# Two streams through a hybrid attention and S5 network on one core: early copies, tiles and splits written ahead of the table steps of a unit, sums' copies ahead of entering states, and the last group's outputs one in a unit

## The chip, the core and the metric

The kernel runs on one core of a Trainium2 chip. The metric is the device time of one execution in microseconds. Of the core's engines TensorE (PE, with its weight loads PEld), VectorE (DVE), ScalarE (ACT), GpSimd (POOL) and SyncE (SP, here only an issuer of DMAs) appear below.

## What is computed

One denoising step over two streams of 128 tokens, width 2048, through two layers. Layer 0 is attention, layer 1 a bidirectional diagonal state-space layer (S5). All weights are float32 and each is used once.

```python
def _pre(x, cond, g, w_ada, b_ada):
    shift, scale, gate = jnp.split(jax.nn.silu(cond) @ w_ada + b_ada, 3, axis=-1)
    h = _rmsnorm(x, g) * (1 + scale) + shift
    return h, gate
...
def _s5_layer(x, cond, p, init, return_state):
    h, gate = _pre(x, cond, g, w_ada, b_ada)
    u, z = jnp.split(h @ w_in, 2, axis=-1)
    ...
    hfr, hfi = _s5_scan(ug, a_re[0], a_im[0], log_dt[0], b_re[0], b_im[0], h0f)
    hbr, hbi = _s5_scan(ug[:, ::-1], a_re[1], a_im[1], log_dt[1], b_re[1], b_im[1], h0b)
    y = _s5_readout(hfr, hfi, c_re[0], c_im[0]) + _s5_readout(hbr, hbi, c_re[1], c_im[1])[:, ::-1]
    y = y.reshape(bsz, l, D_MODEL) + d_skip.astype(jnp.float32) * uf
    y = jax.nn.gelu(y).astype(x.dtype)
    y = y * jax.nn.sigmoid(y @ w_glu + b_glu)
    out = (y * jax.nn.silu(z)) @ w_out
    return x + gate * out
```

## The kernel before

**Units.** The large products (input and output projections of both layers, and the gated linear unit, GLU) are cut into 36 blocks of 512 output columns, and each block into 8 units of 256 input rows, 288 units in all, numbered k. Every engine's program is one Python loop over k, written out, and an engine executes its instructions in just that order. `place(k)` says which block and which of its units stands at k. A unit is 12 matmuls (`products`, lines 821 to 823): for two k tiles and two streams, the weight's high part with the activations' high part, the low part `wlo` with `xhi`, and `whi` with `xlo`.

**Splits.** ACT copies a unit's raw weights to their high part (`split`, line 1095) and DVE subtracts to get the low part (line 1495). From unit 12 on the split of unit k + 4 is written at unit k, and it waits until unit k has been multiplied. Raw weights are loaded by SP, one load for two units, into slots that free as units are multiplied.

**Early steps.** In the first 16 units the modulation of layer 0 is still being computed. TensorE multiplies the chunks of `w_ada` between units (`ada_early`, line 687); ACT copies a finished sum to `adasb` (`adasb_early`, line 1054); TensorE turns it to columns (line 693); DVE makes shift and scale of them and scales a transposed activation tile (`early_tiles`: lines 1481 to 1506), ACT takes its high part (line 1116) and DVE its low part `xlo` (line 1513). Tiles 2c and 2c + 1 are made at the end of unit 4c - 1.

**Table steps.** The tables of the S5 layer are made in 16 quarters n spread over the units by `table_units(n)`: five numbers, the units of `b_bar` (its two `b_table` halves, bt, follow one and two units later), of TensorE's transposes of bt (line 745, two units; ACT stages each half, bs, and stores it), of `c_table` (two units), of the band product (line 762) and of the diagonals.

**S5 steps.** Four groups w of 512 channels, in four quarters q each. `s5_sums` (TensorE line 939, then four ACT copies, lines 1188 and 1189, into sb) makes what a chunk of tokens adds to the state; DVE scans over the chunks; `s5_entering` (four ACT copies, lines 1204 to 1207, from sb into hy) lays out each chunk's entering state, `s5_outputs` (TensorE lines 958 and 962, then a GELU on ACT, line 1217, into ys) gives the outputs. Each sum uses the same two PSUM banks as the one before it, and each output the same one bank, so that TensorE waits for ACT's copies of the sum before (`s_Ssb`) and for ACT's GELU of the output before (`s_ysb`). S_AT, HY_AT and Y_AT are the first units of these steps for each group. A copy into sb of group w + 2 must follow the entering state of the same quarter of group w, which reads the same buffer. A group's outputs go to DRAM and come back transposed (Y, loaded by POOL); `transposed` (line 800) makes the activation tiles of the GLU of it, at the units of the fourth row of X_AT. Blocks 28 to 30 take turns from unit 224 to 247; tiles 6 and 7 are first used by units 242 and 243. After the last group's outputs POOL loads the GLU bias, the gates and the last norm's gains (lines 667, 562 and 670).

Of the kernel before, what the change touches and what calls it, by code (L numbers as in the profile page):

```python
# [57 lines left out]
def table_units(n):  # L58


    if n < 3:
        return ((3, 8, 6, 10, 10), (12, 15, 15, 19, 20), (17, 21, 20, 27, 28))[n]
    if n < 12:
        steps = ((1, 5, 4, 8, 9), (10, 14, 13, 17, 18), (17, 21, 20, 27, 28))[n % 3]
        return tuple(UB * 4 * (n // 3) + u for u in steps)
    steps = ((2, 6, 5, 9, 10), (8, 12, 11, 15, 16), (16, 20, 19, 22, 23), (22, 27, 25, 29, 30))[n - 12]
    return tuple(UB * B_OUT0 + u for u in steps)
# [23 lines left out]
def scan_plan():  # L91
# [4 lines left out]
    for k in range(sums[0], UB * B_END):  # L96
# [20 lines left out]
Y_AT = tuple(x + (4 if w < 2 else 3) for w, x in enumerate(HY_AT))  # L117
# [4 lines left out]
        tuple(UB * B_TURNS + u for u in (-5, -4, -2, 2, 7, 9, 14, 16)),  # L122
# [36 lines left out]
def quarters_at(starts, k):  # L159

    return [(w, q) for w, x in enumerate(starts) for q in range(4) if x + (q // 2 if w == NW - 1 else q) == k]

# [68 lines left out]
def build(nc, d):  # L231
    with ExitStack() as ctx:
# [447 lines left out]
        def _(pe):  # L680
# [286 lines left out]
            def s5_beside(k):  # L967
# [3 lines left out]
                for w, q in quarters_at(Y_AT, k):  # L971
# [35 lines left out]
        def _(act):  # L1007
# [218 lines left out]
            def s5_beside(k):  # L1226
# [6 lines left out]
                for w, q in quarters_at(Y_AT, k):  # L1233
                    s5_outputs(w, q)
                for w, q in quarters_at(HY_AT, k):
                    s5_entering(w, q)
                if s5_at(S_AT, 4, k):
                    s5_sums(*s5_at(S_AT, 4, k))
# [14 lines left out]
            for k in range(NU):  # L1253
# [7 lines left out]
                if u == 0 and ada_beside(b - 1) is not None:  # L1261
# [3 lines left out]
                    af(adasb[:, ada_slot(b)], ps[:, 4], ACT.Copy).then_inc(s_adasb, 1)  # L1265
                if b < B_OUT0:
# [3 lines left out]
                if k < 12 and k % 2 == 1:  # L1270
                    adasb_early(k // 4 + 1, k // 2 % 2)
                if k < 12 and k % 4 == 3:
                    split(k + 1)
                    split(k + 2)
                    early_tiles(k // 4 + 1)
                    split(k + 3)
                    split(k + 4)
# [56 lines left out]
        def _(dve):  # L1334
# [296 lines left out]
            def early_tiles(c):  # L1631
# [4 lines left out]
                modulated(0, 2 * c)  # L1636
                for g in (2 * c, 2 * c + 1):
                    low(0, g)

# [3 lines left out]
            for k in range(NU):  # L1643
# [13 lines left out]
                if k in YZ_AT:  # L1657
# [6 lines left out]
                    dve.wait_ge(s_yz, w + 1)  # L1664
                if b < B_OUT0:
                    attention(b // 4, b % 4, u)
                tables(k)
                if k < 12 and k % 4 == 3:
                    split(k + 1)
                    split(k + 2)  # L1670
                    early_tiles(k // 4 + 1)
                    split(k + 3)
                    split(k + 4)
# [144 lines left out]
```

## Time and profile before

| | |
|---|---|
| median of 3 runs | 1159.76 us (1158.07 to 1163.18) |
| the profiled execution | 1162.38 us |
| its span in the profile | 1160.4 us |
| TensorE busy | 1090.1 us, 94% of the span |
| DVE, ACT, POOL busy | 65%, 49%, 19% |
| mean granted TensorE clock | 0.974 of full speed |

The span runs from the first to the last recorded instruction; what lies around it is 2.0 us. TensorE's busy time is no measure of its speed, since its matmuls overlap. The profile also says for each instruction how long its engine stood idle ahead of it and which instruction of which engine ended that.

### The profile page before, as it was taken

Reading aid. Unit: us, or ns where it says so; the run is one execution under the profiler, and the core shown is the slowest. Engines: PE = TensorE matmul, PEld = TensorE weight load, DVE = VectorE, ACT = ScalarE, POOL = GpSimd, SP = SyncE. Lnnn points to the kernel's source line nnn. Section 1 sums busy time; section 2 is a strip of 40 time slices with the busy share of each in tenths; the row PEclk is TensorE's granted clock in tenths of the full one; section 3 lists DMA queues with packets and bytes.
Section 4 is the critical chain, followed back from the end, with each engine's and each line's share of the span. In section 5 each row is a group of like instructions: output and inputs, shape, how many; then the busy total and the mean of one; then the engine's idle time right before and its main releaser. Section 6 shows DMA issues by size and latency. Waiting matters only on the chain.

```text
span 1160.4 us, 17361 instructions
## 1 busy us (share of the span) xinstructions
PE 1090.1 (94%) x6786; PEld 825.6 (71%) x6786; DVE 757.7 (65%) x1209; ACT 568.8 (49%) x800; POOL 219.2 (19%) x378
## 2 busy tenths in 40 slices
PE   2998899999999999999999989999898998999997
PEld 0455677677777777778777657888686876888885
DVE  4353765766565765677687876369967796476665
ACT  4433434433433444435444346566668586355452
POOL 2010230343122511222134431100020202100000
PEclk9799899999999999999999989999898998999998
DMA  9999687889879997876598867877473767765552
GB/s 372 402 421 419 247 317 267 326 326 346 324 279 377 347 338 261 335 268 224 234 376 336 337 246 290 268 247 238 161 242 122 247 225 273 260 253 181 182 186 104
DMA packets 63457, 325.04 MB, mean 280 GB/s; under 512 B 9392, under 2 KB 16176, under 8 KB 31248
## 3 DMA queue, kind: packets, MB, share of 16 engines
q1 hardware_dynamic: 42800, 265.85, 61.5%
q0 software_dynamic: 12944, 46.94, 11.4%
q10 hardware_dynamic: 7632, 11.15, 2.7%
q8 instruction: 54, 0.88, 0.3%
q14 instruction: 27, 0.22, 0.1%
HBM read 295.55 MB, written 28.34 MB: 279 GB/s over the span
## 4 chain that ended last, share of the span: by engine, by line
PE 76%; DVE 9%; DMA 6%; ACT 6%; issue 3%; ACTq 0%; DVEq 0%
PE ps L821 20%; PE ps L823 18%; PE ps L822 18%; PE ps L687 7%; DMA raw<-in_w 3%; DVE wlo L1495 3%; PE ps L939 2%; ACT whi L1095 2%; PE ps L962 1%; PE ps L800 1%; PE ps L762 1%; DMA araw<-in_wada 1%; DMA gT<-in_gT 1%; PE ps L745 1%; ACT hy L1206 1%
## 5 line engine op out<-in xcount | busy, mean ns | idle before, releaser
L1495 DVE TENSOR_TENSOR wlo<-raw,whi 128x1024 fp32r<-128x1024 f32 x284 | 346.9, 1227 | 291.1 <-ACT whi L1095 286.9
L1095 ACT ACTIVATE whi<-raw 128x1024 fp32r<-128x1024 f32 x284 | 298.3, 1058 | 431.4 <-PE ps L823 403.9
L821 PE MATMUL ps<-whi,xhi 128*128 128x512 f32 x1136 | 465.6, 410 | 6.5 <-DVE xlo L1513 4.6
L822 PE MATMUL ps<-wlo,xhi 128*128 128x512 f32 x1152 | 455.0, 395 | 0.0
L823 PE MATMUL ps<-whi,xlo 128*128 128x512 f32 x1136 | 448.5, 395 | 0.0
L821 PEld LDWEIGHTS ps<-whi,xhi 128*128 128x128 f32 x1136 | 216.6, 191 | 92.7 <-issue 27.9
L823 PEld LDWEIGHTS ps<-whi,xlo 128*128 128x128 f32 x1136 | 216.4, 190 | 48.1
L822 PEld LDWEIGHTS ps<-wlo,xhi 128*128 128x128 f32 x1152 | 220.0, 191 | 41.4
L687 PE MATMUL ps<-araw,cT 128*32 128x512 f32 x640 | 78.6, 606 | 1.9 <-DMA araw<-in_wada 1.9
L687 PE MATMUL ps<-raw,cT 128*32 128x512 f32 x128 | 20.2, 734 | 28.3 <-DMA gT<-in_gT 16.1
L687 PEld LDWEIGHTS ps<-araw,cT 128*32 128x32 f32 x640 | 16.9, 110 | 39.6 <-issue 30.8
L629 POOL DMA_DIRECT2D ctab<-ctab_scratch x16 | 8.6, 541 | 190.8 <-PE ps L962 190.8
L1607 DVE TENSOR_TENSOR t<-coef,sb 128x256 f32<-128x256 f32 x66 | 27.9, 422 | 23.8 <-ACT sb L1189 22.6
L1612 DVE TENSOR_TENSOR sb<-sb,t 128x128 f32<-128x128 f32 x140 | 40.4, 292 | 4.6
L939 PE MATMUL ps<-utf,btab 64*128 64x64 f32 x512 | 35.1, 291 | 8.0 <-ACT sb L1189 8.0
L939 PEld LDWEIGHTS ps<-utf,btab 64*128 64x128 f32 x512 | 32.9, 204 | 13.1 <-issue 12.9
L1513 DVE TENSOR_TENSOR xlo<-ps,xhi 128x512 fp32r<-128x512 f32 x40 | 27.4, 688 | 19.7 <-ACT xhi L1116 19.5
L1116 ACT ACTIVATE xhi<-ps 128x512 fp32r<-128x512 f32 x40 | 23.7, 593 | 29.6 <-DVE ps L1506 19.4
L523 POOL COPY bbf<-bb 64x256 f32<-64x256 f32 x16 | 12.2, 762 | 121.5 <-DVE bb L1410 108.3
L687 PEld LDWEIGHTS ps<-raw,cT 128*32 128x32 f32 x128 | 3.2, 119 | 38.5 <-DMA gT<-in_gT 16.1
L499 POOL DMA_DIRECT2D par<-in_par x16 | 8.7, 547 | 114.3 <-DVE bt L1422 114.0
L531 POOL TENSOR_SCALAR ce<-par 128x128 f32<-128x128 f32 x32 | 28.8, 902 | 2.9
(227 smaller groups left out, 1100.3 us busy)
## 6 DMA issues: line engine op xcount, KB each, us to landing
raw<-in_w SPq DMA_DIRECT2D x144, 1024.0 KB, 5.7
araw<-in_wada SPq DMA_DIRECT2D x80, 1024.0 KB, 8.8
raw<-in_wada SPq DMA_DIRECT2D x16, 1024.0 KB, 9.8
ctab_scratch<-ce POOLq DMA_DIRECT2D x16, 512.0 KB, 8.4
btab_scratch<-bs ACTq DMA_DIRECT2D x32, 256.0 KB, 5.8
btab<-btab_scratch SPq DMA_DIRECT2D x16, 512.0 KB, 3.9
ctab<-ctab_scratch POOLq DMA_DIRECT2D x16, 512.0 KB, 4.8
par<-in_par POOLq DMA_DIRECT2D x32, 128.0 KB, 6.6
```

What stands on the lines that cost most here:

```text
L531: last = nc.gpsimd.tensor_scalar(ce[:, 1, j], par[:, 3], -1.0, None, ALU.mult)
L687: last = mm(ps[32 * j:32 * j + 32, bank], cT32[:, c * CK + j], rhs[:, j * BN:(j + 1) * BN], start=c == 0, stop=c == NCK - 1)
L821: mm(acc, xhi[:, kt, st], hi[:, k], start=kt == 0, stop=False)
L822: mm(acc, xhi[:, kt, st], wlo[:, slot, k0 % 2, k], start=False, stop=False)
L823: last = mm(acc, xlo[:, kt, st], hi[:, k], start=False, stop=kt == KT - 1)
L939: last = mm(ps[:, (4, 7)[e], c0:c0 + M2], btab[h, q, k, ri], utf[h, w, 4 * q + k], start=True, stop=True)
L1095: af(whi_at(k).rearrange("p k c -> p (k c)"), src, ACT.Copy).then_inc(s_hi, 1)
L1116: af(xhi[:, 2 * g:2 * g + 2].rearrange("p k s c -> p (k s c)"), ps[:, x_bank(n)], ACT.Copy).then_inc(s_xhi, 1)
L1495: tt(wlo[:, slot, k % 2].rearrange("p k c -> p (k c)"), src, whi_at(k).rearrange("p k c -> p (k c)").bitcast(F32), ALU.subtract).then_inc( ...
L1513: tt(xlo[:, 2 * g:2 * g + 2].rearrange("p k s c -> p (k s c)"), ps[:, x_bank(n)], xhi[:, 2 * g:2 * g + 2].rearrange("p k s c -> p (k s c)" ...
L1607: last = tt(t, coef[:, w], now.unsqueeze(1).to_broadcast([P, 2, 2, 2 * GW]), ALU.mult)
L1612: last = tt(nxt, nxt, t[:, :, half], ALU.add)
```

## The change

It changes the order in which instructions are written, and no instruction's work:

- In units 1 to 11, the copy of the early sums, the early tiles and the splits are written ahead of the table steps of their unit. On DVE one split now lies between the scaling of the tiles and their low parts; on ACT one split is written ahead of the tiles and three behind them, where there were two and two.
- The table of units for quarter 1 has its first number at 11 where it was 12.
- On ACT, `s5_sums`' copies are written ahead of `s5_entering` of the same unit.
- The last group's outputs start at unit 231, one in a unit up to 234 (they were two at unit 230 and two at 231), and tiles 6 and 7 of the GLU are transposed at units 241 and 242 (they were at 238 and 240).

```diff
--- before.py
+++ after.py
@@ -59,7 +59,7 @@
 
 
     if n < 3:
-        return ((3, 8, 6, 10, 10), (12, 15, 15, 19, 20), (17, 21, 20, 27, 28))[n]
+        return ((3, 8, 6, 10, 10), (11, 15, 15, 19, 20), (17, 21, 20, 27, 28))[n]
     if n < 12:
         steps = ((1, 5, 4, 8, 9), (10, 14, 13, 17, 18), (17, 21, 20, 27, 28))[n % 3]
         return tuple(UB * 4 * (n // 3) + u for u in steps)
@@ -114,12 +114,12 @@
 
 
 S_AT, HY_AT, SCAN = scan_plan()
-Y_AT = tuple(x + (4 if w < 2 else 3) for w, x in enumerate(HY_AT))
+Y_AT = tuple(x + (4, 4, 3, 4)[w] for w, x in enumerate(HY_AT))
 
 
 X_AT = ((), tuple(UB * B_OUT0 + u for u in (-4, -2, -1, 1, 1, 2, 3, 4)),
         tuple(UB * B_IN1 + u for u in (0, 0, 0, 1, 2, 3, 4, 5)),
-        tuple(UB * B_TURNS + u for u in (-5, -4, -2, 2, 7, 9, 14, 16)),
+        tuple(UB * B_TURNS + u for u in (-5, -4, -2, 2, 7, 9, 17, 18)),
         tuple(UB * B_OUT1 + u for u in (-6, -5, -4, -3, -2, -1, 3, 4)))
 X_BANK = ((5, 6, 5, 6, 5, 6, 5, 6), (4, 4, 7, 7, 5, 6, 7, 5), (6, 7, 5, 6, 7, 5, 6, 7), (5, 7, 4, 7, 7, 7, 7, 7),
           (7, 5, 6, 7, 5, 6, 7, 5))
@@ -159,6 +159,11 @@
 def quarters_at(starts, k):
 
     return [(w, q) for w, x in enumerate(starts) for q in range(4) if x + (q // 2 if w == NW - 1 else q) == k]
+
+
+def outputs_at(k):
+
+    return [(w, k - x) for w, x in enumerate(Y_AT) if 0 <= k - x < 4]
 
 
 def ahead(k):
@@ -968,7 +973,7 @@
 
                 if k in U_AT:
                     s5_transposed(U_AT.index(k))
-                for w, q in quarters_at(Y_AT, k):
+                for w, q in outputs_at(k):
                     s5_outputs(w, q)
                 if s5_at(S_AT, 4, k):
                     s5_sums(*s5_at(S_AT, 4, k))
@@ -1230,12 +1235,12 @@
                 if k in U_AT:
                     for i in range(2):
                         s5_transposed(U_AT.index(k), i)
-                for w, q in quarters_at(Y_AT, k):
+                for w, q in outputs_at(k):
                     s5_outputs(w, q)
+                if s5_at(S_AT, 4, k):
+                    s5_sums(*s5_at(S_AT, 4, k))
                 for w, q in quarters_at(HY_AT, k):
                     s5_entering(w, q)
-                if s5_at(S_AT, 4, k):
-                    s5_sums(*s5_at(S_AT, 4, k))
                 if k == Y_AT[NW - 1] + 4:
                     act.wait_ge(s_fsT, 1)
                     act.wait_ge(s_y, 4 * NW)
@@ -1263,18 +1268,17 @@
                     if ada_order(b) > 2:
                         act.wait_ge(s_adafin, fins(b - 1))
                     af(adasb[:, ada_slot(b)], ps[:, 4], ACT.Copy).then_inc(s_adasb, 1)
+                if k < 12 and k % 2 == 1:
+                    adasb_early(k // 4 + 1, k // 2 % 2)
+                if k < 12 and k % 4 == 3:
+                    split(k + 1)
+                    early_tiles(k // 4 + 1)
+                    for x in range(k + 2, k + 5):
+                        split(x)
                 if b < B_OUT0:
                     attention(b // 4, b % 4, u)
                 tables(k)
                 s5_beside(k)
-                if k < 12 and k % 2 == 1:
-                    adasb_early(k // 4 + 1, k // 2 % 2)
-                if k < 12 and k % 4 == 3:
-                    split(k + 1)
-                    split(k + 2)
-                    early_tiles(k // 4 + 1)
-                    split(k + 3)
-                    split(k + 4)
                 if u == UB - 1:
                     if b < B_GLU and not B_OUT0 <= b < B_IN1:
                         act.wait_ge(s_wused, k + 1)
@@ -1628,15 +1632,17 @@
                         if step == NCH - 1:
                             scanned(w)
 
-            def early_tiles(c):
+            def early_tiles(c, unit=None):
+
                 dve.wait_ge(s_adaE, c + 1)
                 cols = [ps[:, 7, 16 * c + 8 * i:16 * c + 8 * i + 8].rearrange("p (k s) -> p k s", s=NS) for i in range(2)]
                 shift_or_scale(cols, 0, c, 4 * c, 4, s_adaEout)
                 dve.wait_ge(s_adaEout, c + 1)
                 modulated(0, 2 * c)
+                if unit is not None:
+                    split(unit)
                 for g in (2 * c, 2 * c + 1):
                     low(0, g)
-
             for k in range(4):
                 split(k)
             early_tiles(0)
@@ -1662,15 +1668,13 @@
                     cols = slice(w * BN, (w + 1) * BN)
                     tt(WA[:, :, cols], WA[:, :, cols], Y[:, :, cols], ALU.mult).then_inc(s_yz, 1)
                     dve.wait_ge(s_yz, w + 1)
+                if k < 12 and k % 4 == 3:
+                    early_tiles(k // 4 + 1, k + 1)
+                    for x in range(k + 2, k + 5):
+                        split(x)
                 if b < B_OUT0:
                     attention(b // 4, b % 4, u)
                 tables(k)
-                if k < 12 and k % 4 == 3:
-                    split(k + 1)
-                    split(k + 2)
-                    early_tiles(k // 4 + 1)
-                    split(k + 3)
-                    split(k + 4)
                 if u == UB - 1:
                     if B_OUT0 <= b < B_IN1:
                         if b == B_OUT0:
```

On DVE, the piece around the end of unit 11 (in the changed kernel line numbers are 4 or 5 higher). Names are tiles: wlo is the low part of a split, shT, modt and gsT the shift and scale, xlo a tile's low part, bands the diagonals of unit 10, bb the first table step of quarter 1. Before:

```order
L1495 TENSOR_TENSOR wlo<-raw,whi 128x1024 x2
L1481 TENSOR_TENSOR shT<-ps,bT 128x8
L1484 TENSOR_TENSOR modt<-ps,bT 128x8
L1486 SCALAR_TENSOR_TENSOR gsT<-modt,gT 128x8
L1506 TENSOR_SCALAR ps<-ps,gsT,shT 128x128 x4
L1513 TENSOR_TENSOR xlo<-ps,xhi 128x512 x2
L1495 TENSOR_TENSOR wlo<-raw,whi 128x1024 x3
L1405 TENSOR_TENSOR bb<-ff,par 128x128
```

and now:

```order
L1458 TENSOR_TENSOR bands<-bands,ps 128x2x16
L1459 TENSOR_TENSOR bands<-bands,dm 128x2x16
L1485 TENSOR_TENSOR shT<-ps,bT 128x8
L1488 TENSOR_TENSOR modt<-ps,bT 128x8
L1490 SCALAR_TENSOR_TENSOR gsT<-modt,gT 128x8
L1510 TENSOR_SCALAR ps<-ps,gsT,shT 128x128 x4
L1499 TENSOR_TENSOR wlo<-raw,whi 128x1024
L1517 TENSOR_TENSOR xlo<-ps,xhi 128x512 x2
L1499 TENSOR_TENSOR wlo<-raw,whi 128x1024 x3
L1409 TENSOR_TENSOR bb<-ff,par 128x128
```

The two splits that stood ahead of the shift and scale are behind them, one of them between the scaling and the low parts.

On ACT, at units 207 and 208 (S5 groups 1 and 3). hy is an entering state, sb what the sums' copies write, WA the SiLU of the evacuated block. Before:

```order
L1095 ACTIVATE whi<-raw 128x1024
L1204 ACTIVATE hy_109<-h_113 64x16x2
L1205 ACTIVATE hy_109<-h_113 64x16x2
L1206 COPY hy_109<-sb 64x16x62
L1207 COPY hy_109<-sb 64x16x62
L1188 COPY sb<-ps 64x2x4x32x2
L1189 COPY sb<-ps 64x2x4x32x2
L1188 COPY sb<-ps 64x2x4x32x2
L1189 COPY sb<-ps 64x2x4x32x2
```

and now:

```order
L1100 ACTIVATE whi<-raw 128x1024
L1193 COPY sb<-ps 64x2x4x32x2
L1194 COPY sb<-ps 64x2x4x32x2
L1193 COPY sb<-ps 64x2x4x32x2
L1194 COPY sb<-ps 64x2x4x32x2
L1209 ACTIVATE hy_109<-h_113 64x16x2
L1210 ACTIVATE hy_109<-h_113 64x16x2
L1211 COPY hy_109<-sb 64x16x62
L1212 COPY hy_109<-sb 64x16x62
```

The four copies into sb have changed places with the four copies into hy.

On ACT, units 229 to 233: ys is the GELU of one quarter's outputs, xhi a tile's high part. Before:

```order
L1095 ACTIVATE whi<-raw 128x1024 x2
L1217 ACTIVATE ys<-ps 128x4x64 x2
L1116 ACTIVATE xhi<-ps 128x512
L1095 ACTIVATE whi<-raw 128x1024
L1217 ACTIVATE ys<-ps 128x4x64 x2
L1223 DMA y_scratch<-ys 128x1x256 x4
L1095 ACTIVATE whi<-raw 128x1024
L1116 ACTIVATE xhi<-ps 128x512
```

and now:

```order
L1100 ACTIVATE whi<-raw 128x1024 x2
L1121 ACTIVATE xhi<-ps 128x512
L1100 ACTIVATE whi<-raw 128x1024
L1222 ACTIVATE ys<-ps 128x4x64
L1100 ACTIVATE whi<-raw 128x1024
L1222 ACTIVATE ys<-ps 128x4x64
L1121 ACTIVATE xhi<-ps 128x512
L1100 ACTIVATE whi<-raw 128x1024
L1222 ACTIVATE ys<-ps 128x4x64
L1100 ACTIVATE whi<-raw 128x1024
L1222 ACTIVATE ys<-ps 128x4x64
L1228 DMA y_scratch<-ys 128x1x256 x4
```

Between two GELUs there is now a split in every case, and the tile of unit 231 and three splits stand ahead of the first.

## Rows read from the trace of the kernel before

**Rows 1.** The page: the span, and three groups of instructions.

```profile
span 1160.4 us, 17361 instructions
L1495 DVE TENSOR_TENSOR wlo<-raw,whi 128x1024 fp32r<-128x1024 f32 x284 | 346.9, 1227 | 291.1 <-ACT whi L1095 286.9
L1095 ACT ACTIVATE whi<-raw 128x1024 fp32r<-128x1024 f32 x284 | 298.3, 1058 | 431.4 <-PE ps L823 403.9
L1513 DVE TENSOR_TENSOR xlo<-ps,xhi 128x512 fp32r<-128x512 f32 x40 | 27.4, 688 | 19.7 <-ACT xhi L1116 19.5
```

**Rows 2.** Timeline of the early stage: start, length in us, engine, line, operation, idle before.

```profile
103.94 0.60 ACT L1054 ACTIVATE adasb<-ps 128x512 f32<-128x512 f32 x1 [0.46 <-ACT bs L1065]
...
104.59 1.92 PE L687 MATMUL ps<-raw,cT 128*32 128x512 f32 x16 [2.63 <-ACT adasb L1054]
...
113.05 1.87 PE L693 MATMUL ps<-sel,adasb 128*128 128x2 f32 x16
...
117.51 1.37 DVE L1506 TENSOR_SCALAR ps<-ps,gsT,shT 128x128 f32<-128x128 f32 x4
...
120.35 0.79 PE L821 MATMUL ps<-whi,xhi 128*128 128x512 f32 x1 [2.56 <-DVE xlo L1513]
...
127.09 0.28 DVE L1405 TENSOR_TENSOR bb<-ff,par 128x128 f32<-128x128 f32 x1
...
135.59 0.66 PE L745 MATMUL ps<-ident,bt 128*128 128x128 f32 x4 [2.66 <-DVE bt L1422]
```

**Rows 3.** Engines by stretch: busy us (count), then TensorE's granted clock, DMA share, GB/s.

```profile
110.00:115.00 5.00, 5.00 (x61) 3.56 (x50) 0.62 (x3) 2.35 (x5) 0.00 (x0) 1.00 1.02 425
833.50:840.30 6.80, 6.80 (x41) 5.97 (x41) 6.29 (x17) 6.64 (x11) 0.00 (x0) 0.51 0.23 78
980.20:987.00 6.80, 5.12 (x56) 4.66 (x57) 3.81 (x4) 2.52 (x5) 0.00 (x0) 0.50 0.12 51
```

**Rows 4.** Groups of instructions of the stretch from 820 to 1000 us.

```profile
L1206 ACT COPY hy<-sb 64x992 f32<-64x992 f32 x16 | 17.4, 1089 | 0.2
L1205 ACT ACTIVATE hy<-h 64x32 f32<-64x32 f32 x16 | 3.7, 229 | 0.2
```

**Rows 5.** Timeline of the sums and entering states.

```profile
833.25 1.08 PE L939 MATMUL ps<-utf,btab 64*128 64x64 f32 x8 [3.58 <-ACT sb L1189]
...
841.48 1.06 ACT L1095 ACTIVATE whi<-raw 128x1024 fp32r<-128x1024 f32 x1 [1.10 <-PE ps L823]
...
852.43 0.38 ACT L1217 ACTIVATE ys<-ps 128x256 f32<-128x256 f32 x1
...
891.04 3.42 PE L939 MATMUL ps<-utf,btab 64*128 64x64 f32 x32 [2.00 <-ACT sb L1189]
...
899.25 1.06 ACT L1095 ACTIVATE whi<-raw 128x1024 fp32r<-128x1024 f32 x1 [2.29 <-PE ps L823]
```

**Rows 6.** Timeline: starts of units 212, 213, 229 and 230, then the last outputs.

```profile
907.39 0.50 PE L821 MATMUL ps<-whi,xhi 128*128 128x512 f32 x1
...
912.05 0.50 PE L821 MATMUL ps<-whi,xhi 128*128 128x512 f32 x1
...
969.31 0.39 PE L821 MATMUL ps<-whi,xhi 128*128 128x512 f32 x1
...
972.03 0.39 PE L821 MATMUL ps<-whi,xhi 128*128 128x512 f32 x1
...
979.47 1.06 ACT L1095 ACTIVATE whi<-raw 128x1024 fp32r<-128x1024 f32 x1
...
981.88 1.12 PE L958 MATMUL ps<-kd,utf 64*64 64x64 f32 x16 [5.28 <-ACT ys L1217]
...
1002.10 0.47 PE L821 MATMUL ps<-whi,xhi 128*128 128x512 f32 x1
```

**Rows 7.** DMAs issued from 999 to 1007 us: count, KB, us from issue to landing.

```profile
gfin<-in_g_fin POOLq DMA_DIRECT2D x1, 1024.0 KB, 21.5
raw<-in_w SPq DMA_DIRECT2D x1, 1024.0 KB, 12.0
```

## The prediction

> **What bounds the kernel now.** The page's engine table shows TensorE busy almost throughout, but its matmuls overlap, so the first view that says something is the timeline of TensorE with the idle time ahead of each instruction. One unit of 12 matmuls takes 969.31 to 972.03 = 2.72 us when nothing waits, and a unit with an S5 output behind it 907.39 to 912.05 = 4.66, so an output costs 1.94 [rows 6]. The 288 units alone are 288 x 2.72 = 783 us of the span of 1160.4 [rows 1]. What a new order can win is the time in which TensorE waits, and it does so in three places that this change touches:
>
> A, the early stage: 2.63 us for the copy adasb, 2.56 for the low part of tile 6, 2.66 for the bt table [rows 2].
> B, the sums: 3.58 at 833.25 and 2.00 at 891.04, both for ACT's copies sb [rows 5].
> C, the last outputs: 5.28 at 981.88 for the GELU ys [rows 6].
>
> The second view is the table by stretches, for the clock. TensorE was granted 0.51 of full speed, 1.2 instead of 2.4 GHz, from 833.5 to 840.3, right after the 3.58 us wait, and 0.50 from 980.2 to 987.0, around the 5.28 us wait [rows 3]. So a long wait is paid twice: 6.8 us at half speed, all of it worked through, is 3.4 us lost. The wait of 2.63 us at 104.59 [rows 2] was not followed by it: 110 to 115 shows 1.00 [rows 3].
>
> **The change part by part.** No instruction is added or removed; every term is a wait that gets shorter or longer.
>
> *A.* On ACT the copy adasb at 103.94 goes ahead of one staged copy and the wait on it, 0.60 + 0.46 = 1.1 us [rows 2], so TensorE's wait of 2.63 becomes 1.5 and the columns (113.05, 1.87 long) end at 113.8 instead of 114.9. DVE scaled the tile at 117.51 only because two splits of 1.23 each [rows 1] stood ahead of it; now it starts on the columns, and with half a microsecond for the three small operations the scaling runs from 114.4 to 115.8. Then one split (1.23) while ACT takes the high part, and the low part (0.69, rows 1 again): 117.7, where TensorE started unit 12 at 120.35. That is 2.6 us. DVE then owes, up to the end of the second bt half: a low part 0.69, three splits 3.7, the six small operations that begin at 127.09 (0.28 each, 1.7), and two splits and two halves of three 0.69 operations, 2.5 + 4.1; with about 1.1 of waits on ACT's parts, 13.8 us: 131.5, against 135.59 [rows 1, 2]. TensorE waits there still, about 2.5 us, but 4.0 earlier. Term A is **4.0**. It rests on DVE, which has nothing idle in that stretch; were the copy's 1.1 lost, it is 3.0; if the half-speed stretch after the wait disappears as well (a bt wait of 2.5 is near the 2.63 that did without), up to 5.4. The lower bound is 0: from 110 to 115 the DMA engines are full (share 1.02, 425 GB/s) [rows 3], and if the weights of units 12 to 15 land no earlier than they are used now, nothing moves. I keep 4.0, because DVE made the splits of 12 and 13 before 117.51, so that those weights were there; what moves is work done after they land.
>
> What pays for A: the second half of `c_table` for quarter 0 goes behind the splits of units 10 and 11 on DVE, to about 105.5 (these splits end near 103.4, and it is three operations of 0.69). TensorE's band product needs it at the end of unit 10, about 108: a cover of 2 to 3 us, and one for one beyond it. The first `b_bar` moves behind splits too, and POOL, which fills ce and issues loads, is later by up to 20 us; it is next needed at unit 15, near 131.
>
> *B, groups 0 and 2 (units 197 to 201).* An entering state is two copies of 1.09 and two of 0.23 [rows 4], 2.7 us with the gaps. With the sums' copies ahead of it, the sum that TensorE began at 833.25 can begin at 830.6. But ACT is the bound here: it is busy 98% of the stretch at 833.5 [rows 3], and up to the GELU that ends at 852.43 + 0.38 = 852.81 its one pause is the 1.10 us at 841.48 in which it waited for TensorE [rows 5]. TensorE's second output needs that GELU. All work is the same in a new order, so only the 1.1 us go: TensorE gains 2.7 at first and gives back all but **1.1** at unit 201. Without the half speed TensorE is at that output some 4 us earlier and released 1.1 earlier, so a wait of about 2.9 arises there. Bounds: +1.2, and 3.4 less, -2.2, if half speed follows it.
>
> *B, groups 1 and 3 (units 207 to 211).* The copies that released TensorE at 891.04 end 2.7 us earlier. Here ACT has room: its split at 899.25 waited 2.29 us for TensorE [rows 5], and more behind it, so the gain stays. The half-speed time I leave as it is: the first wait of this stretch goes, but the other grows to about 3.6 us. Term **2.7**, bounds 2.3 (ACT's room) and 6.0 (one stretch at half speed, 3.4, less).
>
> Behind the copies of sums stand the entering states, 2.5 us later; outputs read them four units later, more than 10 us, which covers it.
>
> *C.* From the start of unit 230 (972.03) to that of unit 235 (1002.10) it is 30.1 us [rows 6]. Without waits: five units 13.6, four outputs 7.8, two tiles' transposes of at most the 0.66 of the four at 135.59 [rows 2], say 0.8 for both: 22.2. The new order asks the first GELU of ACT later: after 979.47 two splits (2.1), the tile's high part 0.6, a split 1.06, the GELU 0.38, 983.5. TensorE reaches the second output at 972.03 + 3 x 2.72 + 1.94 + 0.4 = 982.5, and waits 1.0. The next two outputs have a full unit ahead of them, 2.7 us, where a split and a GELU take 1.5. So 23.2 instead of 30.1: 6.9 gained. Against it, tiles 6 and 7 are now transposed right ahead of the last unit before the ones that use them. For tile 7, DVE has behind unit 241: a high part 1.06 (ACT), a split 1.23, the product of WA and Y over 1024 columns 1.2, its low part 0.69, together 4.2; unit 242 with its transposes is 3.1. TensorE waits 1.1 at unit 243. Term C is **5.8**. Bounds: 6.9 if that wait is covered; 3.7 if the weights of unit 244, whose split stands ahead of tile 6 on ACT, take the 12.0 us of a load issued under the POOL loads [rows 7] instead of about 10: then tile 6 is late too.
>
> Sum: 4.0 + 1.1 + 2.7 + 5.8 = 13.6 us, against the profiled execution's own 1162.38 (span 1160.4, 2.0 around it): 1148.8. That execution lies 2.6 above the median of the runs, 1159.76, so the median should be **1146.2**.
>
> **A rule weighed.** The rows say that after 3.58 us of waiting the clock was 0.51, and after 2.63 us still 1.00. The Trainium skill, "TensorE: Matmul & The Clock Gate", part 1 on the clock gate, has it that the throttled state is the default and that only activity releases it, on a grid of time that does not start with the kernel. By that, which of two similar waits is punished is chance. By the rows, the sum keeps as much half-speed time in A and B as now; by the rule, the waits left in B (2.4, 2.9 and 3.6 us) could each bring one. That is the second rival.
>
> **The rivals.**
> 1. *ACT and DVE are the bound and only hand the wait on.* In B and A no work is taken from them. For it: ACT's one pause of 1.1 us ahead of 852.81. Against it: 2.29 us of pause at 899.25 [rows 5]. If B gives nothing, 1162.4 - 9.8 = 1152.6, median 1150.0; if A gives nothing instead (loads late, share 1.02), 1149.9 to 1150.2. Chance 0.22 for either.
> 2. *The waits stay long enough to halve the clock each time.* In B two more stretches of 6.8 us, 3.4 us each less the waits that they shorten, take back term B's 3.8 and up to 2 more: median 1150 to 1152. Chance 0.10. The skill's clock page, same part, is behind this one.
> 3. *A table step or tile becomes the wait.* c_table behind the splits in A, or tiles 6 and 7 in C, late by 8 us together: median within 0.5% of now, 1154 to 1158. Chance 0.10.
> 4. *Slower.* POOL's loads (Y, bias, gates, gains: 4.5 MB) are issued as now when the last outputs are stored, which is two to three units later in the order of units. gfin took 21.5 us to land among them [rows 7]. If the weights of unit 244 landed like that and not like the 12.0 us, tile 6 would wait behind the split on ACT for 9 us more. Against the 10 us assumed, each us to landing costs one: from 24 us on the 13.6 are gone, and at 32 us the median is 1168. Against it: weights come on another queue and took 12.0 at the height of that traffic. Chance 0.03. The Trainium skill, "DMA: Bandwidth & Descriptors", on queues, rings and completion order, says that a DMA engine takes turns between the queues that have work; the two rows of group 7 agree.
>
> **How the numbers follow.** The forecast has 0.55, its own range 1142 to 1149. Rivals 1 and 2 reach to 1153, and its upper ends (A 5.4, B 1.2 + 6.0, C 6.9, 19.5 in all) to 1140: the range is 1140 to 1153, and leaves out rivals 3 and 4 and some of the tail. A change of 0.5%, 5.8 us, is about what a measurement of this kernel tells from none. Faster by more: 0.55 + 0.22 + 0.10 = 0.87; within it: rival 3, 0.10; slower by more: 0.03.
>
> **What would show it.** A: unit 12 starts near 117.8, the bt wait ends near 131.5. B: the sum after unit 198 starts 2.7 earlier relative to its unit, then TensorE waits nearly 3 us for the GELU at the output of unit 201; ACT shows no pause between. At unit 210 ACT's wait for TensorE is gone or short. C: outputs one a unit, a wait of about 1 us at the second, clock 1.00 around it, and a wait of about 1 us at unit 243. The prediction is wrong if half-speed stretches move to 848 to 855, if the wait for xlo at 242 or 243 is over 3 us with a weight load ahead of it, or if the band product at unit 10 waits for ce.

## The result, and the profile after

The kernel after takes 1156.08 us (median of 20 runs, 1149.81 to 1161.92), the kernel before, run beside it, 1160.63 (20 runs, 1158.07 to 1164.45). The ratio is 0.9948, interval 0.9936 to 0.9960: 6.0 us less, not 13.6. It is outside the range, and it lies where rival 3 was put (1154 to 1158). The runs after spread over 12 us, those before over 6. That made me look for two cases among the executions, but by itself it proves nothing: 29 runs of the kernel before in the first set of experiments spread over 11.7 us (1156.10 to 1167.76).

The profiled execution took 1160.52 us, 4.4 above the median, so it is one of the slower executions. Its page begins so:

```profile
span 1158.7 us, 17360 instructions
PE 1087.1 (94%) x6786; PEld 822.4 (71%) x6786; DVE 757.3 (65%) x1209; ACT 568.3 (49%) x800; POOL 216.5 (19%) x378
```

**Place A.** The timeline of TensorE (start, length, line, and in brackets the idle time ahead and what ended it): unit 12, and the transposes of bt ahead of unit 16.

```profile
116.45 0.50 PE L826 MATMUL ps<-whi,xhi 128*128 128x512 f32 x1 [0.99 <-DVE xlo L1517]
...
133.20 1.11 PE L750 MATMUL ps<-ident,bt 128*128 128x128 f32 x4 [5.22 <-DVE bt L1426]
```

Unit 12 starts at 116.45 where it started at 120.35 [rows 2]: 3.9 us, even more than forecast. But the wait for bt ends at 133.20 instead of 135.59: 2.4 us of it are kept, and the wait has grown from 2.66 to 5.22. ACT and DVE in the same stretch show why:

```profile
125.64 2.01 ACT L1100 ACTIVATE whi<-raw 128x1024 fp32r<-128x1024 f32 x2 [5.61 <-DMA raw<-in_w]
```

```profile
122.95 0.29 DVE L1414 TENSOR_TENSOR bb<-bb,m 128x128 f32<-128x128 f32 x1
126.80 1.23 DVE L1499 TENSOR_TENSOR wlo<-raw,whi 128x1024 fp32r<-128x1024 f32 x1 [3.56 <-ACT whi L1100]
127.94 0.69 DVE L1419 TENSOR_TENSOR bt<-pw,bb 128x512 f32<-128x512 f32 x1
...
132.46 0.69 DVE L1426 TENSOR_TENSOR bt<-bt,m 128x512 f32<-128x512 f32 x1
```

ACT's split of unit 16 waited 5.61 us for its weights, DVE's half of that split waited for ACT, and the first half of `b_table`, which needs neither, stands behind it. DVE is idle 3.56 us between `b_bar` and the split: the pause that the prediction said was not there. The load of these weights, in the stretch from 110 to 113.2 of before and of after (KB, us to landing):

```profile
raw<-in_w SPq DMA_DIRECT2D x1, 1024.0 KB, 11.6
...
raw<-in_w SPq DMA_DIRECT2D x1, 1024.0 KB, 15.3
```

It was asked for at 110.31 where it was asked for at 112.62, and yet it landed later, at 125.62 instead of 124.27: in this stretch, where the DMA engines are full [rows 3], asking sooner did not bring it sooner.

**Place B.** Two rows of TensorE, an output behind unit 201 and a sum behind unit 209:

```profile
850.47 0.68 PE L963 MATMUL ps<-kd,utf 64*64 64x64 f32 x16 [2.58 <-ACT ys L1222]
...
887.41 0.91 PE L944 MATMUL ps<-utf,btab 64*128 64x64 f32 x6 [3.44 <-ACT sb L1194]
```

The waits are those forecast, 2.9 and 3.6.

**Place C.** TensorE's outputs of the last group, tile 7's transposes and unit 242, then ACT and DVE just ahead of them:

```profile
976.56 0.68 PE L963 MATMUL ps<-kd,utf 64*64 64x64 f32 x16
...
981.22 0.68 PE L963 MATMUL ps<-kd,utf 64*64 64x64 f32 x16
...
986.25 0.68 PE L963 MATMUL ps<-kd,utf 64*64 64x64 f32 x16
...
1017.90 1.09 PE L805 MATMUL ps<-ident,Y 128*128 128x128 f32 x4 [5.20 <-DVE xlo L1517]
1018.64 0.78 PE L826 MATMUL ps<-whi,xhi 128*128 128x512 f32 x1
```

```profile
1014.84 1.06 ACT L1100 ACTIVATE whi<-raw 128x1024 fp32r<-128x1024 f32 x1 [6.91 <-DMA raw<-in_w]
1015.80 0.58 ACT L1121 ACTIVATE xhi<-ps 128x512 fp32r<-128x512 f32 x1
```

```profile
1015.93 1.23 DVE L1499 TENSOR_TENSOR wlo<-raw,whi 128x1024 fp32r<-128x1024 f32 x1 [6.74 <-ACT whi L1100]
1017.07 0.68 DVE L1517 TENSOR_TENSOR xlo<-ps,xhi 128x512 fp32r<-128x512 f32 x1
```

The outputs wait for nothing any more, where the kernel before waited 5.28 us [rows 6]. Then the split of unit 244 waits for its weights, the high and low part of tile 6 stand behind it on both engines, tile 7 needs tile 6's bank, and TensorE waits 5.20 us. POOL's issues and the issues by line of two short stretches (KB, us to landing) tell what was ahead of those weights:

```profile
999.08 0.71 POOL L650 DMA_DIRECT2D Y<-y_scratch  x1 [29.46 <-DMA y_scratch<-ys]
999.84 0.56 POOL L672 DMA_DIRECT2D bglu<-in_b_glu  x1
```

```profile
bglu<-in_b_glu POOLq DMA_DIRECT2D x1, 1024.0 KB, 8.6
...
raw<-in_w SPq DMA_DIRECT2D x1, 1024.0 KB, 13.5
```

The weights were asked for at 1001.36, 1.5 us behind POOL's load of bglu, and landed 13.5 us later. Last the windows (length, busy time and count of each engine, granted clock, DMA share, GB/s) behind the three waits and around the outputs:

```profile
131.90:138.70 6.80, 5.50 (x16) 4.48 (x17) 5.66 (x7) 1.68 (x3) 4.30 (x7) 0.52 0.22 77
...
852.10:855.50 3.40, 3.40 (x16) 2.66 (x13) 2.66 (x8) 2.01 (x3) 0.53 (x1) 0.54 0.46 142
...
977.00:990.00 13.00, 13.00 (x174) 10.69 (x170) 9.51 (x9) 6.68 (x10) 0.00 (x0) 1.00 0.60 234
1015.90:1022.70 6.80, 4.80 (x14) 4.02 (x15) 4.78 (x5) 2.02 (x3) 0.00 (x0) 0.52 0.70 292
```

The half speed of before at the outputs [rows 3] is gone, and stands behind the three new waits shown here instead.

### The profile page after: what moved, and what is told of

It reads as the page before. It is cut to its first block, busy times and chain, and to the rows that moved or that the text cites. A ratio compares the mean times of both kernels' runs of the same rounds, so it can differ in the third digit from the quotient of the medians.

```text
span 1158.7 us, 17360 instructions
## 1 busy us (share of the span) xinstructions
PE 1087.1 (94%) x6786; PEld 822.4 (71%) x6786; DVE 757.3 (65%) x1209; ACT 568.3 (49%) x800; POOL 216.5 (19%) x378
## 3 DMA queue, kind: packets, MB, share of 16 engines
q0 software_dynamic: 12944, 46.94, 11.5%
## 4 chain that ended last, share of the span: by engine, by line
PE 72%; DMA 10%; DVE 8%; ACT 6%; issue 3%; ACTq 0%; DVEq 0%; SPq 0%
PE ps L826 19%; PE ps L828 18%; PE ps L827 18%; PE ps L692 7%; DMA raw<-in_w 4%; DVE wlo L1499 3%; DMA araw<-in_wada 2%; DMA raw<-in_wada 2%; ACT whi L1100 2%; PE ps L967 1%; PE ps L805 1%; PE ps L750 1%; PE ps L767 1%; DMA gT<-in_gT 1%; PE ps L944 1%
## 5 line engine op out<-in xcount | busy, mean ns | idle before, releaser
L805 PEld LDWEIGHTS ps<-ident,WA 128*128 128x128 f32 x128 | 16.4, 152 | 14.3 <-issue 10.8
```

Source lines behind the costliest of these rows:

```text
L805: last = tr(ps[:, x_bank(n), (2 * k + st) * P:(2 * k + st + 1) * P], src[:, st, (2 * g + k) * P:(2 * g + k + 1) * P], ident[:])
```

## The experiments

### The three parts, each alone

Each kernel is the one before with one part of the diff of the change: A (the order in the ACT and DVE loops, `b_bar` at 11), B (`s5_sums` ahead of `s5_entering` on ACT), C (`Y_AT`, `outputs_at`, and the last two entries of the tiles' row).

```diff
A -    return ((3, 8, 6, 10, 10), (12, 15, 15, 19, 20), ...
A +    return ((3, 8, 6, 10, 10), (11, 15, 15, 19, 20), ...   and early copies, tiles, splits ahead of tables(k)
B +                if s5_at(S_AT, 4, k): s5_sums(...)           ahead of the loop over s5_entering
C -        tuple(UB * B_TURNS + u for u in (-5, -4, -2, 2, 7, 9, 14, 16)),
C +        tuple(UB * B_TURNS + u for u in (-5, -4, -2, 2, 7, 9, 17, 18)),   and outputs_at(k)
```

> The kernel before with part A alone (early copies, tiles and splits ahead of the table steps, first b_bar at unit 11 instead of 12). The prediction's term says 4.0 us less than before (ratio 0.9966). Theory 1, that the gain of units 12 to 15 (3.9 to 5.0 us in the trace of after) is handed to a wait for the second bt half, which stands on DVE behind the split of unit 16 whose weights land at 125.6: 1.0 to 2.0 us (0.9983 to 0.9991), with a wait of over 4 us at the transposes of bt behind unit 15 and unit 17 some 1.5 us earlier. Theory 2, that what is lost there is one unlucky half-speed stretch: 4 to 5 us in the median of the runs, and in a profile without half speed after that wait.

> The kernel before with part B alone (copies of the sums ahead of the entering states on ACT). The prediction's term says 3.8 us less (0.9967). Theory 1, from the trace of after, where units 199 to 203 gave back all but -0.4 us of the 2.7 and units 207 to 211 kept 1.8: 1 to 2 us (0.998 to 0.999). Theory 2, half speed by chance: the two places differ between executions, and the median comes near 3.8.

> The kernel before with part C alone (last group's outputs one in a unit, tiles 6 and 7 ahead of units 241 and 242). The prediction's term says 5.8 us less (0.9950). Theory 1: the outputs give 6.7 us as forecast, and the transposes of tile 7 ahead of unit 242 then wait over 4 us for the low part of tile 6, which stands on ACT and DVE behind the split of unit 244, whose weights land late; with the half speed behind that wait, all of it is given back: -1.5 to +1.5 us (0.9987 to 1.0013). Theory 2, that the weights' landing varies with what the POOL queue does and this part on its own leaves the units later against the loads: 3 to 6 us less.

| part | ratio to before, interval | us, from the ratio | forecast |
|---|---|---|---|
| A | 0.9985, 0.9974 to 0.9997 | 1.7 (0.3 to 3.0) | 4.0 |
| B | 0.9977, 0.9963 to 0.9990 | 2.7 (1.2 to 4.3) | 3.8 |
| C | 0.9998, 0.9981 to 1.0015 | 0.2 (-1.7 to 2.2) | 5.8 |

Together 4.6 of the 6.0. A keeps its wait for bt, 4.08 us long:

```profile
132.64 0.69 PE L745 MATMUL ps<-ident,bt 128*128 128x128 f32 x2 [4.08 <-DVE bt L1421]
```

B fits its forecast within its interval, but 2.7 lies between the two theories named ahead of it (1 to 2, and near 3.8) and doesn't choose. C alone gives nothing in the ratio, but its 12 runs go from 1156.40 to 1164.72, and the profiled one is the quickest of them: there no wait stands ahead of unit 242, and the issue of the weights of unit 244, in a stretch at 1002.5, reads

```profile
raw<-in_w SPq DMA_DIRECT2D x1, 1024.0 KB, 4.8
```

POOL's bias load was issued at 1004.17 there, behind the weights. So the second theory, which expected the landing to vary, had a point, but not in the median, where the first has its number. From here on the question was that order.

### Tile 6 ahead of the split of unit 244

```diff
     last = UB * (B_END - 1)
+    if k in (240, 241):
+        return () if k == 240 else (244, 245)
     if k < last - 2:
```

> The kernel after with one exchange on ACT and DVE: the split of unit 244 stands behind the parts of tile 6 instead of ahead of them. The loads are not touched. Theory 1 (tile 6 was late only because it stood behind a split that waited 6.9 us for its weights): the wait of 5.2 us ahead of unit 242 goes or is under 1 us, unit 244 waits little, and the time is 5 to 8.5 us below that of after (0.993 to 0.9955 of it; 0.988 to 0.990 of before). The rival, that the weights are late for the units themselves: the wait moves to unit 244 or 245 and under 2 us are gained.

1154.79 us (6 runs, 1150.45 to 1157.73), ratio 0.9942, interval 0.9923 to 0.9962: 0.7 us below after, within the noise. The first theory asked for 5 to 8.5. Its profile (1150.93) happened to have the weights issued just ahead of POOL's loads too, so it could not tell; the forced pair below could.

### The same kernel, two more profiled executions

> The kernel after unchanged, one more profiled execution. If the order of the loads is what differs between executions of it: either POOL's loads are issued ahead of the weights of unit 244, these take over 11 us and unit 242 waits over 4 us, or behind them, these take about 5 us and no wait stands at unit 242, and the time is then 5 us or more below 1160.5. If the order is the same in every execution, the wait of 5.2 us is there again.

> The same as the look before, a third profiled execution of the kernel after.

1149.24 and 1150.75 us, with the kernel after unchanged. Of the first of these two (the second execution in the table below), TensorE ahead of unit 242 and what preceded it on ACT, and the issues of a stretch at 996.2:

```profile
1007.53 0.63 PE L805 MATMUL ps<-ident,Y 128*128 128x128 f32 x4
1007.91 0.47 PE L826 MATMUL ps<-whi,xhi 128*128 128x512 f32 x1
```

```profile
1004.47 1.06 ACT L1100 ACTIVATE whi<-raw 128x1024 fp32r<-128x1024 f32 x1 [1.66 <-PE ps L828]
1005.43 0.58 ACT L1121 ACTIVATE xhi<-ps 128x512 fp32r<-128x512 f32 x1
```

```profile
raw<-in_w SPq DMA_DIRECT2D x1, 1024.0 KB, 4.8
```

These weights were issued at 996.24, POOL's bglu at 997.37. No wait for tile 6, no half speed from 1003 to 1012. From the start of unit 241 to that of unit 243 it is 13.57 us in the first profile (1009.69 to 1023.26) and 7.35 in this one (1004.56 to 1011.91): 6.2 us, wait and half speed together, between the two orders of the loads within one kernel. The third execution has the same order, the good one with the weights ahead (weights at 997.17, bglu at 998.49). Part by part, by how much earlier than in the profile of before the units start (at unit 17; from there to 230; from 230 to 243):

| execution of after | A | to unit 230 (B) | C | sum |
|---|---|---|---|---|
| first, 1160.52 us | 1.6 | 1.4 | -1.2 | 1.7 |
| second, 1149.24 us | 3.2 | 4.1 | 5.7 | 13.1 |
| third, 1150.75 us | 4.2 | 3.1 | 4.8 | 12.1 |
| forecast | 4.0 | 3.8 | 5.8 | 13.6 |

So sums near the forecast's do occur in the quick executions; 5 of the 20 runs behind the median are below 1153 us. But each row is a difference of two single executions, and that of before was a slow one (1162.38). The profiles of B alone and C alone, which lack part A, start unit 17 also 1.6 and 2.0 us ahead of it. So this table does not show that A gives 3.2 or 4.2 us; only the terms of B and C come near their size by it.

The order of the two loads seems to hang on the last store of ys, for whose landing POOL's first load waits. In the first execution that store was issued at 995.24, ahead of the load of the weights of unit 242 (995.67), and landed 3.4 us later. In the second and third it was issued at 990.78 and 991.75, behind that load (990.55 and 991.48), and landed after 5.4 and 5.5 us, and POOL's loads with it came later. Of the other seven profiles with part C six fit this; in C alone the store was 0.2 us ahead of the load and took 6.3. No run forces this pair, so it is not shown to be the cause.

### The order of the loads, forced both ways

The first edit, on POOL, puts its loads of bias, gates and gains behind the weights of unit 244 (the load of Y stays ahead of them); the second, on SP, makes the weights wait until the last quarter of Y has landed, which puts them behind the issue of all of POOL's loads; the third is the second with the exchange of tile 6 and the split as above.

```diff
(later)   pool.wait_ge(s_y, 4 * NW)
(later)  +pool.wait_ge(s_wused, 239)
(later)   pool.dma_start(bglu[:], ...
(behind) +if g == 122:
(behind) +    sp.wait_ge(s_yin[3], 16)
(behind)  slot = w_slot(g)[0]
```

> The kernel after with one wait more on POOL: its loads of the bias, the gates, the gains and the store of the state wait until unit 238 is done, so that they are issued behind the load of the weights of units 244 and 245 and not just ahead of it. Theory (the traces of after, of C alone and of the run with tile 6 first differ in this order, by chance of when the store of the last output lands: with POOL's loads ahead the weights took 13.5 us, with them behind 4.7 and 4.8): the load takes about 5 us in every run, the wait ahead of unit 242 is gone, the runs lose their upper part, and the median is 3 to 5 us below that of after (ratio to before 0.990 to 0.992). The rival, that the spread comes from half-speed stretches elsewhere: the median stays within 1.5 us of after's.

> The kernel after with the load of the weights of units 244 and 245 forced behind POOL's loads (SP waits until the last quarter of Y has landed). If the order of these loads decides, this is the bad case in every run: the weights take 10 to 14 us, unit 242 waits 6 to 9 us for the low part of tile 6, part of it is followed by half speed, and the median is 3 to 6 us above after's (ratio to before 0.998 to 1.000). The rival, that it does not matter: within 1.5 us of after.

> The same forced order of loads, and the parts of tile 6 ahead of the split of unit 244 on ACT and DVE. If tile 6 was late only by its place behind the split, the wait ahead of unit 242 goes although the weights are as late; what is left is a wait of unit 244 itself, which starts about 5 us later: under 4 us, and the median is 3 to 6 us below that of the forced order alone. The rival, that the load is late for the units themselves whatever the order on ACT: under 2 us between the two.

| kernel | median us | ratio to before, interval | us less than before |
|---|---|---|---|
| after | 1156.08 | 0.9948, 0.9936 to 0.9960 | 6.0 |
| POOL's loads later | 1151.14 | 0.9920, 0.9905 to 0.9936 | 9.3 |
| weights behind | 1157.63 | 0.9968, 0.9955 to 0.9980 | 3.7 |
| weights behind, tile 6 first | 1158.32 | 0.9978, 0.9963 to 0.9993 | 2.6 |

The two kernels that differ from after by one wait each, on POOL or on SP, lie 5.6 us apart, and the kernel after lies between, as a mixture of the two orders should. The first is within what was expected; the second is 2.3 us above after where 3 to 6 were expected. The second edit also delays the weights themselves: they were asked for at 1006.22, 6 us behind the start of unit 238, and not at once as in after, so its wait is a longer one than the plain order makes. With POOL's loads later, the weights landed in 5.3 us and no wait stands ahead of unit 242. With the weights behind, TensorE waited 7.88 us; that row, and the row of the fourth kernel that takes its place:

```profile
1019.67 0.66 PE L807 MATMUL ps<-ident,Y 128*128 128x128 f32 x2 [7.88 <-DVE xlo L1519]
```

```profile
1026.26 0.79 PE L830 MATMUL ps<-whi,xhi 128*128 128x512 f32 x1 [4.52 <-DVE xlo L1521]
```

With tile 6 first, unit 242 starts without a wait and unit 243 waits 4.52 us for tile 7, which stands behind the splits of units 244 and 245 and is followed by half speed (0.67 from 1026 to 1031). In the median nothing is gained, where 3 to 6 us were expected. So by the medians the late landing costs as much with tile 6 ahead of the split as behind it. The profiles don't agree with that in full: from the start of unit 241 to that of unit 245 it is 21.67 us with the weights behind and 17.72 with tile 6 first, against 12.93 with POOL's loads later. The profile with tile 6 first is the slowest of its 12 runs (1165.04) and also has a wait of 5.38 us for Y ahead of unit 231, which is not part of the edit. Whether the exchange is worth something when the weights are late stays open; that their landing is what costs is shown by the first two edits.

### Both halves of b_table at once, ahead of the split of unit 16

```diff
-                        if k == units[0] + 1 + ri:
+                        if k == units[0] + (0 if n == 1 else 1 + ri):
                             b_table(n, ri)
```

> The kernel after with both halves of b_table of the second quarter right behind its b_bar on DVE at unit 11, ahead of the split of unit 16. Theory: the wait of 4 to 5 us at the transposes of bt behind unit 15 is not work of DVE but bt standing behind a split whose weights land at 125.6: it goes to under 1 us, unit 17 starts 3 to 4 us earlier than in after, and with a stretch at half speed less up to 3 us more; the time is 2 to 5 us below after (0.990 to 0.993 of before). The rival, that the early stage is bound by the DMA engines (share 1.0): the wait moves to the units 16 to 20 for their weights and under 1 us is gained.

> The kernel before with part A, and the two halves of b_table at unit 11, right behind the b_bar. Part A alone gave a ratio of 0.9985. If the place of bt behind the split of unit 16 took part A's gain, this one gives 5.3 us more, 7.0 us or 0.9940, and the trace shows no wait at the transposes of bt and full speed from 125 to 145. If the early stage hands the wait on to later weights: 0.997 to 0.9985.

On the kernel after: 1149.61 us, ratio 0.9902, interval 0.9886 to 0.9918, 5.3 us below after. On part A alone: 1153.84 us, ratio 0.9941, interval 0.9923 to 0.9959, the 0.9940 expected: 6.9 us from part A where it gave 1.7. The rival, a stretch bound by the DMA engines, falls: ACT still waited 5.93 us for the weights of unit 16, but no wait of TensorE followed from it. DVE's rows of the first kernel, TensorE's and two windows:

```profile
124.21 0.29 DVE L1414 TENSOR_TENSOR bb<-bb,m 128x128 f32<-128x128 f32 x1
124.54 0.69 DVE L1419 TENSOR_TENSOR bt<-pw,bb 128x512 f32<-128x512 f32 x1
...
128.20 0.69 DVE L1426 TENSOR_TENSOR bt<-bt,m 128x512 f32<-128x512 f32 x1
128.93 1.22 DVE L1499 TENSOR_TENSOR wlo<-raw,whi 128x1024 fp32r<-128x1024 f32 x1
```

```profile
129.06 0.60 PE L750 MATMUL ps<-ident,bt 128*128 128x128 f32 x4
130.29 0.47 PE L826 MATMUL ps<-whi,xhi 128*128 128x512 f32 x1 [0.64 <-ACT qkvz L1137]
```

```profile
120.00:130.00 10.00, 9.66 (x44) 7.54 (x43) 9.72 (x16) 4.07 (x6) 2.20 (x3) 1.00 0.89 361
130.00:140.00 10.00, 9.71 (x49) 8.06 (x50) 9.86 (x12) 7.13 (x11) 5.50 (x7) 1.00 0.72 248
```

The six operations of bt fill the time in which DVE waited, the transposes start at 129.06 without a wait (133.20 in after), and the clock stays at 1.00. So the gain is the wait and the half speed behind it; the runs don't part the two.

### Both edits together

> The kernel after with both edits that helped: the two halves of b_table right behind the b_bar at unit 11, and POOL's loads behind the load of the weights of unit 244. If the two losses are apart, their gains over after (5.3 and 3.3 us by the ratios) add: 8.6 us below after, ratio to before 0.9872, and a median near 1147. If the gain of the first came only because units then met POOL's loads at another moment, they don't add: 0.989 to 0.991.

1146.87 us (6 runs, 1144.03 to 1152.36), ratio 0.9889, interval 0.9864 to 0.9913: 12.9 us below before and 6.8 below after. The sum of the two, 8.6, is within the interval, and so is a loss of 2 us in the combination; these runs don't decide between them. The ratio expected if they add was 0.9872. It has the lowest median of the study and is clear of after, but not of the kernel with bt at once alone (ratio 0.9902), whose interval overlaps. That its median is about the predicted one is chance: it is another kernel.

## Why the prediction was wrong

**C, the step that failed most.** "3.7 if the weights of unit 244, whose split stands ahead of tile 6 on ACT, take the 12.0 us of a load issued under the POOL loads [rows 7] instead of about 10". The mechanism was named and its row read; its size was wrong twice. The weights took 13.5 us, so that TensorE waited 5.2 us for tile 6 where that sentence has about 2; and I gave that wait no half speed, though from 1015.9 to 1022.7 the clock was 0.52 with TensorE busy 4.80 us of it, so about 2.4 us more (half speed costs half of the busy time only). The term that the sum used, a landing of about 10 us, stands in no row: in the profile of before the load asked for at the start of unit 238 took 11.5 us. One figure for the landing was also the wrong idea: issued ahead of POOL's load of bglu the weights took 4.7 to 6.4 us in the profiles, behind it 10.4 to 13.5. The outputs themselves gave what was forecast: from unit 230 to unit 235 the profiles differ by 6.6 us (2.9 earlier at 230, 9.5 at 235), forecast 6.9. In the executions with the weights ahead, the only wait behind them is the 1.0 us at unit 243, as forecast (1.1). What decides is something that I had written under rival 4 as fixed, "issued as now when the last outputs are stored": in the profile of before POOL's loads were issued from 999 on and unit 238, at whose start the weights of unit 244 are asked for, began at 1010.75; in after unit 238 begins at 1001.17 and POOL's loads are still issued at 999 to 1001. The 9.5 us gained by the units brought the two together. With the good order forced, 9.3 us are gained; less A's 1.7 and B's 2.7, measured alone, that leaves 4.9 for C, of 5.8.

**A.** "It rests on DVE, which has nothing idle in that stretch" was wrong. The forecast let DVE work through its 13.8 us; after 122.95 it had work, but the next instruction in its order was a split whose weights had not landed. I had looked at the landing of the weights of units 12 to 15 (correctly: unit 12 gained 3.9 us) and not of unit 16, which landed no sooner (125.62, before 124.27) though all else had moved ahead. The first profile kept 2.4 us of 4.0, the wait grew to 5.22, and half speed (131.9 to 138.7) followed it; alone, the part gave 1.7. In the other two executions the wait for bt is 4.2 us as well and A's gain at unit 17 is 3.2 and 4.2, with as much half speed or half of it, so part of A's spread is the clock's. The edit with bt at once takes both away.

**B.** Right within what can be told: 2.7 (1.2 to 4.3) for 3.8. The waits were 2.58 and 3.44 for 2.9 and 3.6. Whether group 0 and 2 give 1.1 or lose hung on the clock: in the first profile half speed followed the wait of 2.58, and unit 203 starts 0.9 us earlier than before, where unit 198 started 1.6 earlier: a loss of 0.7. In the third execution of the same kernel the wait was 2.63 and 848 to 856 ran at 1.00.

**The rule weighed.** The forecast rested on one wait that was not punished, 2.63 us and then 1.00 [rows 3]. The profile of before has two more of that length in the same stage, 2.56 us at 120.35 and 2.66 at 135.59 [rows 2], and both went the other way:

```profile
120.00:123.30 3.30, 2.95 (x7) 2.38 (x8) 1.74 (x3) 3.27 (x6) 0.00 (x0) 0.50 1.01 416
137.00:140.40 3.40, 3.40 (x9) 2.52 (x8) 1.79 (x3) 1.08 (x2) 2.86 (x5) 0.50 0.36 121
```

So "a bt wait of 2.5 is near the 2.63 that did without" was no ground for a bound. Of the kernel after the rows say: 2.58 us of wait, then clock 0.54; 2.63 us at the same place in another execution, then 1.00. The Trainium skill, "TensorE: Matmul & The Clock Gate", part 1, has it that the grid is not tied to the kernel's start, so that the same wait may or may not be punished; the traces agree. I gave that rival 0.10 and left the forecast's half-speed time as it was, which was too kind for a change that leaves waits of 2.5, 2.9 and 3.6 us.

**The rivals.** Rival 3 came true in its time and in one of its two places, tiles 6 and 7; the other, `c_table`, didn't show: no wait for ce or at the band product. That its time was hit is in part luck: of the 7.6 us missing, 2.3 are A's and 1.1 B's, by the parts measured alone, and neither is a tile or `c_table` that came late. It should have had more than 0.10, since two steps of the sum named the same suspect. Rival 1's "loads late" is half of A. Rival 4 had the right transfer and overrated it.

## What to carry to other kernels

- When work is moved ahead, look past the wait that it removes for the next load that the sooner consumers ask for, and for everything that stands in order behind its first reader on each engine. Work that needs no load goes ahead of a split that does: here that was worth 5.3 us for one line.
- A load's time to landing is not one number but depends on which queue asked first. Where two queues issue within a few us of each other, price both orders, and put a wait that fixes the good one. A second profiled execution of the same kernel can show such a race; the spread of the runs alone can't, since the kernel before spread over 6 us in one set and 12 in another.
- Before blaming the place behind a waiting instruction, force the bad case and exchange the two: here the exchange gained nothing in the median.
- A part read off one pair of profiles carries the luck of both: compare it with the profile of a kernel that lacks the part.

## What the runs showed of the hardware

A load of 1 MB issued 1.1 us ahead of POOL's load of bglu took 4.8 us, one issued 1.5 us behind it 13.5. The DMA queues of the first profile (packets, MB, share of the 16 engines) show why, first from 1001.4 to 1005, then from 1007 to 1011. POOL's queue is q0, that of the weights q1:

```profile
q0 software_dynamic: 210, 1.22, 95.3%
...
q0 software_dynamic: 69, 1.11, 65.0%
q1 hardware_dynamic: 73, 0.60, 36.2%
```

The weights were asked for at 1001.36, and up to 1005 their queue moved nothing. Then both moved, with as many packets each (69 and 73), but those of POOL's loads are twice as large (1.11 MB in 69, 0.60 in 73), so that the weights got 35% of the bytes. The Trainium skill, "DMA: Bandwidth & Descriptors", on queues, rings and completion order, says that a DMA engine takes turns between its queues packet by packet. From 1007 to 1011 the trace agrees by packets. By bytes the turns are not even, and the first 3.6 us are no turns at all; why the weights' queue began so late is not shown by these runs. With the weights ahead it had the engines to itself: from 998 to 1000 of the second execution it moved 0.79 MB in 2 us where it moved 0.60 in 4 here.

```profile
q1 hardware_dynamic: 96, 0.79, 95.5%
```

So a weight load behind a burst on the other queue is to be priced by the late start and by its share of the bytes, not by its own size.
